# Key factors taken before the seventh combination, the first key transposes one group later, and one weight tile held for six low parts

## What is computed

```python
# layer 0
z = rms_norm(x) @ w_in                       # combined projection
a = pool_mixer(z[..., :512])                 # trailing means, 4 groups
for each of 4 heads:                         # differential attention
    q, k = rope(rms_norm(q)), rope(rms_norm(k))      # two maps of 64 channels each
    p1, p2 = softmax(mask(q1 @ k1.T)), softmax(mask(q2 @ k2.T))
    o = rms_norm((p1 - lam * p2) @ v) * (1 - lam_init)
x = x + concat(a, o) @ w_out
x = x + conv_ffn(x)                          # 1024 -> 2*2816 -> conv, gate -> 1024
# layer 1
q, k = silu(causal_conv(rms_norm(x) @ w_qk))
for each of 4 heads, 8 chunks of 128 tokens:         # mLSTM, matrix memory
    num  = (q @ k.T * decay_matrix) @ [v, 1] + (q * scale) @ state
    state = decay * state + k_weighted.T @ [v, 1]
h = rms_norm(num / max(|den|, exp(-m))) * sigmoid(o)
x = x + h @ w_out
x = x + conv_ffn(x)
```

## Time and profile before

| | |
|---|---|
| median of three runs | 2274.3 us (2273.61 to 2274.34) |
| the profiled execution's own time | 2274.28 us |
| its span, first to last instruction | 2272.5 us |
| TensorE busy | 2261.0 us, 99% |
| its weight loads | 1870.7 us, 82% |
| VectorE busy | 1190.7 us, 52% |
| ScalarE busy | 572.2 us, 25% |
| GpSimd busy | 882.0 us, 39% |

### The profile page before, as it was taken

One profiled execution on the slowest core, in us unless ns is written; L12 is line 12 of the kernel. 1 busy time (PEld: TensorE's weight loads), 2 busy tenths in 40 slices (PEclk: granted clock), 3 DMA queues, 4 the chain that ended last, 5 costly groups with the idle time before them and its releaser, 6 DMA issues.

```text
span 2272.5 us, 27216 instructions
## 1 busy us (share of the span) xinstructions
PE 2261.0 (99%) x10747; PEld 1870.7 (82%) x10747; DVE 1190.7 (52%) x1176; ACT 572.2 (25%) x888; POOL 882.0 (39%) x395
## 2 busy tenths in 40 slices
PE   9999999999999999999999999999999999999999
PEld 7777778888888888888888898788888888888887
DVE  7776763464554555545644144444545555554554
ACT  5555441221111111111344333422111111111110
POOL 1212226444334433344643333275344433443342
PEclk9999999999999999999999999999999999999999
DMA  5111121111111111111321111031111111111111
GB/s 195 56 47 47 33 92 57 47 47 49 54 46 46 46 54 47 46 47 53 115 79 56 35 59 65 21 135 45 51 47 46 46 55 46 46 46 52 50 47 74
DMA packets 38721, 132.29 MB, mean 58 GB/s; under 512 B 4912, under 2 KB 6768, under 8 KB 38640
## 3 DMA queue, kind: packets, MB, share of 16 engines
q1 hardware_dynamic: 35760, 122.24, 16.7%
q10 hardware_dynamic: 2880, 8.91, 1.0%
HBM read 118.26 MB, written 8.68 MB: 56 GB/s over the span
## 4 chain that ended last, share of the span: by engine, by line
PE 95%; DVE 3%; issue 1%; ACT 0%; DMA 0%; SPq 0%; ACTq 0%; DVEq 0%
PE pj L1367 42%; PE dn L1387 17%; PE pj L347 15%; PE pj L325 6%; PE pj L1860 3%; PE dn L1438 3%; PE dn L686 1%; PE pj L712 1%; PE pj L1438 1%; PE pj L506 1%; PE pj L696 1%; PE dn L1998 1%; PE dn L2007 1%; PE dn L1886 1%; PE pj L1886 1%
## 5 line engine op out<-in xcount | busy, mean ns | idle before, releaser
L1661 POOL TENSOR_TENSOR w_hi<-w_raw,ones 128x1024 fp32r<-128x1024 f32 x186 | 356.0, 1914 | 1329.9 <-PE pj L1367 564.0
L1663 POOL TENSOR_TENSOR w_lo<-w_raw,w_hi 128x1024 fp32r<-128x1024 f32 x186 | 468.3, 2518 | 14.6
L1491 DVE SCALAR_TENSOR_TENSOR ffn_y<-ffn_h,params,ffn_y 128x1024 f32<-128x1024 f32 x176 | 323.6, 1838 | 117.6 <-ACT ffn_y L1499 109.0
L1499 ACT ACTIVATE ffn_y<-ffn_h,params 128x1024 f32<-128x1024 f32 x88 | 109.6, 1245 | 886.6 <-DVE ffn_h L1480 886.6
L1480 DVE TENSOR_TENSOR ffn_h<-pj,rms_bc 128x1024 f32<-128x1024 f32 x88 | 107.8, 1225 | 365.5 <-PE pj L1367 351.9
L1540 DVE TENSOR_TENSOR res<-dn,res 128x1024 f32<-128x1024 f32 x144 | 176.1, 1223 | 115.4 <-PE dn L1387 115.4
L1367 PE MATMUL pj<-xb_hi,w_hi 128*128 128x512 f32 x704 | 216.9, 389 | 0.0
L1367 PE MATMUL pj<-xa_hi,w_hi 128*128 128x512 f32 x704 | 216.9, 389 | 0.0
L1367 PE MATMUL pj<-xb_hi,w_lo 128*128 128x512 f32 x704 | 216.7, 389 | 0.0
L1367 PE MATMUL pj<-xa_hi,w_lo 128*128 128x512 f32 x704 | 216.7, 389 | 0.0
L1367 PE MATMUL pj<-xa_lo,w_hi 128*128 128x512 f32 x704 | 216.7, 389 | 0.0
(11 more groups left out here) (321 smaller groups left out, 3550.4 us busy)
## 6 DMA issues: line engine op xcount, KB each, us to landing
w_raw<-weights SPq DMA_DIRECT2D x189, 512.0 KB, 3.5
x_first<-x_t SPq DMA_DIRECT2D x8, 512.0 KB, 9.8
res<-x_t SPq DMA_DIRECT2D x8, 512.0 KB, 6.8
scratch<-res ACTq DMA_DIRECT2D x8, 512.0 KB, 2.6
res<-scratch SPq DMA_DIRECT2D x8, 512.0 KB, 8.4
y_t<-res ACTq DMA_DIRECT2D x7, 512.0 KB, 2.6
q_turned<-q_raw SPq DMA_DIRECT2D x16, 128.0 KB, 2.3
k_turned<-k_raw SPq DMA_DIRECT2D x16, 128.0 KB, 2.3
```

The lines of the kernel that those rows point to most:

```text
L1491: dve.scalar_tensor_tensor(y[:, :], h[:, SH - lag:SH - lag + S], f.tap(j, m, q), y[:, :], ALU.mult, ALU.add).then_inc(taps[f.l], 1)
L1499: act.activation(f.y[m][:, :], f.h[m][:, SH:SH + S], ACT.Identity, bias=f.tap(j, m, 3), scale=f.tap(j, m, 2)).then_inc(center[f.l], 1)
L1661: pool.tensor_tensor(whi[:, w, :], raw[:, r, :], ones[:, 0:1].to_broadcast([P, D]), ALU.mult).then_inc(w_high, 1)
L1663: pool.tensor_tensor(wlo[:, w, :], raw[:, r, :], whi[:, w, :].bitcast(F32), ALU.subtract).then_inc(w_ready, 1)
```

## The change

Three edits, each independent of the others.

1. In `dve_mixer0`, for heads 0 to 2, `dve_KB` of half 0 of the next head moves from the head of block 7 (before its mask) to block 6, just before `dve_combine`.
2. In `pe_layer1`, `pe_KT` of head 0 is issued behind the seventh of the eight leading groups and no longer behind the sixth.
3. In `pool_layer1`, POOL waits, before it cuts tile T_OUT1 + 2, until `cat_lo[1]` has counted six low parts.

```diff
@@ dve_mixer0
                 for i in range(TB):
                     between, middle, after = block_groups(h, i)
-                    if i == TB - 1 and not last:
-                        dve_KB(dve, h + 1, 0)
                     dve_mask(dve, h, i)
@@
                     for G in between + middle + early:
                         extras(G)
+                    if i == TB - 2 and not last:
+                        dve_KB(dve, h + 1, 0)
                     dve_combine(dve, h, i)
@@ pe_layer1
                 for G in range(LEAD[h]):
                     pe_mix1_group(pe, *side1(h, G))
-                    if h == 0 and G == 5:
+                    if h == 0 and G == 6:
                         pe_KT(pe, 0)
@@ pool_layer1
+                if n == T_OUT1 + 2:
+                    pool.wait_ge(cat_lo[1], EARLY_CAT)
                 pool_cut(pool, n, n, 16 * (n // RAW_RING + 1))
```

## The result

The changed kernel takes 2278.24 us (median of 17 runs, 2277.81 to 2279.55) against 2273.89 us (17 runs, 2273.60 to 2274.34): 4.35 us more, a ratio of 1.002 with a 95% interval of 1.0014 to 1.0027. The forecast was 2276.6 us and "no change". The time lies inside the stated range, but the kernel did become slower, and the likeliest case missed 1.6 us of it. The profiled execution took 2279.19 us with a span of 2277.4 us, 4.9 us more than the 2272.5 of before; it is one of the slower of the 17.

A forecast was written before the change was run, and what follows sets the result against it. TensorE matmul work was taken to bound the kernel (95% of the chain that ended last). Terms 0 + 0.7 + 1.6 = +2.3 us on the profiled execution's 2274.28 gave 2276.6 us, range 2274.0 to 2278.4.

The forecast's parts named there:

- the likeliest case: Whole kernel: the terms for the three edits sum to +2.3 us, giving 2276.6 us; chance 60%.
- Part 1: Attention, heads 0 to 2: the 0.48 us wait for key factors goes, but the wait for `w_T` grows; sum 0.
- the term: Block 7 in attention: load about 0.35 us earlier, the 0.48 less about 0.1 of ordinary gap behind turns.
- Part 2: Start of the mLSTM, head 0: later key turns delay the chain to chunk 0's numerator, without slack; +0.7 us.
- Part 3: End of mLSTM head 3: low parts gain 1.3 us, POOL's cut in its new place costs 2.84; net +1.6 us.
- the 4.58 us of the earlier trace: Start of the program: time of the first 20 matmuls, 0.23 us each; about half taken as a clock fall's cost, +2.3.
- the hold pays: End of head 3: small DVE operations pass between POOL's two instructions, or POOL starts later; 2273.7 us, chance 10%.
- the factors or the late turns pay: Heads 0 to 2: 0.35 us three times, 2275.6 us; mLSTM start: chain has slack, 2275.5 to 2275.9; 10% each.
- the clock rival: Turns at head 3's end: after 4.4 us idle, first matmuls run at 1.2 GHz; +2.3 us, 2278.9; chance 10%.
- The bound of 4.5 us: Whole kernel: 0.2%, what a measurement can tell from no change; slower meant above 2278.8 us.
- The 5% for slower: Whole kernel above 2278.8 us: half of the clock rival's 10%, as its time lies just on that edge.

The follow-up runs named there:

- the fill: 18 extra matmuls, result not used, on TensorE's queue ahead of head 3's numerator's turns: changed kernel 2276.48 us, kernel before with three extra DVE operations 2277.04 us.
- the two filled kernels: Changed kernel, and kernel before with three extra DVE operations, each with 18 unused matmuls ahead of head 3's numerator's turns: 2276.48 and 2277.04 us.
- part 3 alone: Kernel before with only the weight tile held until six low parts are counted: 2277.94 us, ratio 1.0019.
- the longer wait: Kernel before with three extra DVE operations (about 3.1 us) ahead of the last operation on head 3's numerator, POOL unchanged: 2279.01 us, ratio 1.0024.
- the full change filled: Changed kernel with 18 extra matmuls, result not used, ahead of head 3's numerator's turns: 2276.48 us, ratio 1.0012.
- parts 1 and 2 alone: Kernel before with only the earlier key factors: 2273.89 us; kernel before with only the first key turns one group later: 2274.49 us.
- the second group: Unchanged kernel before, 33 runs timed beside the second group of experiment kernels: median 2273.96 us.
- both gains together: Kernel before with the tile held for all eight low parts and head 3's numerator's turns one group later: 2271.69 us, ratio 0.999.

## Why the prediction was wrong, step by step

- **Part 1, 0 us: right.** The gain was lost at the next wait, as said; that wait grew by 0.5 us, not 0.35, because no gap at all is left behind the turns of the key factors (the term had allowed 0.1). The time at which the wait ends did not move.
- **Part 2, +0.7 us: right.** 0.64 in the profiled execution, 0.68 by itself. The chain behind the turns had no slack.
- **Part 3, +1.6 us by the cut's new place: right in kind, 0.3 short.** The price of the cut was 6.02 - 3.14 = 2.88 us (2.84 forecast, from the end of head 1). The gain was 1.0 us and not 1.3. The mis-sized term is how much of chunk 7's earlier end reaches ACT's last high parts: 0.4 us by my estimate, 0.26 measured (they ended at 1462.97, which is 1462.3 without the shift of 0.67, against 1462.56 before). DVE stood 0.61 and 0.55 us for high parts and `m_out_gate` followed the last one by 1.56 us, not 1.5. With the clock held, the tile cost 2.0 us.
- **The clock: the step that failed.** I had worked out that TensorE would stand about 4.4 us, and it stood 4.41. That close a match was luck: without the shift the turns came 1.86 us late and not 1.5, and TensorE arrived 1.16 us early and not 1.5. I had a price as well: 2.3 us, half of the 4.58 us of the earlier trace rows. It was 2.35 in the profiled execution, 1.6 and 1.7 in two other traces, and 1.8 and 2.0 by the medians of two kernels with and without the fill. What the traces show in place of the earlier trace rows is half of the time that TensorE works at the low clock, 4.9 us in one and 3.4 in two. But I gave the fall 10% as a rival and left it out of the sum, because the granted clock was 1.00 with waits of up to 1.4 us and, as I read it, the trace held none above 1.48. It held one of 1.89 us on the weight loads, at 9.37 us, also at 1.00, but none near 4.4. That the rows did not show a fall was no evidence against it: they did not reach there. With the term in, the sum is 2274.28 + 0.7 + 1.6 + 2.3 = 2278.9 us, which is 0.7 us above the median of 2278.24, and the forecast would have been "slower". The rule of the Trainium skill ("TensorE: Matmul & The Clock Gate", Part 1: the idle engine's clock falls to the lower level) stood in the prediction and was the better guide. The traces agree in all three cases with an idle time above 4 us: 4.41, 4.41 and 4.67. All 38 runs of these three kernels have a mean granted clock of 0.998 or 0.999, and all 22 of the two filled kernels 1.000; and none of the 38 runs of the full change, of part 3 alone and of the longer wait was as fast as the median of its filled counterpart (part 3 alone is compared with the full change filled, which carries part 2's 0.68 us as well, so the comparison is generous to it).
- **The other rivals.** That the hold pays did not come about, because the small operations were held up just as at the end of head 1; with the tile held to the eighth low part it did pay, 1.0 us. That the factors or the late turns pay was refuted by parts 1 and 2 alone.
- **The range** of 2274.0 to 2278.4 held the median by 0.2 us at its upper end, by luck: it was drawn to leave out most of the clock rival, 2278.9, and that rival is what came, 0.7 us cheaper. The bound of 4.5 us, under which a change could not be told from none, was wrong too: 4.35 us is told apart, with an interval of 1.0014 to 1.0027. The 5% for slower rested on both.

Why POOL's cut stops DVE: the Trainium skill, "SBUF — State Buffer", section "SBUF: two separate sides", says that VectorE and GpSimd share one pair of ports, that an instruction holds it to its end, and that the other engine is fully blocked, where the VectorE operation reads two inputs from SBUF or uses both ports. The trace agrees: an operation on 8 columns took 2.25 us and ended with POOL's, while `m_out_gate`, one of whose inputs is in PSUM, took 1.22 us beside the cut and 1.21 without it.

## What to carry to other kernels

A transfer of work away from a critical stretch must name where it lands: a wait that is released by the last step of one critical stretch starts its work on the first step of the next. Of a wait on the bounding engine that grows, ask at once whether it is longer than any in the trace, and put the fall of its clock into the sum, not beside it; if the wait can't be shortened, real work moved into it is best, and even useless work gave back 1.8 and 2.0 us here. And when an order changes by one group, check each later point at which another engine's work is released by that engine's progress, not only the waits nearby.

## What the runs showed that I had not expected

That 18 matmuls whose result is thrown away made the changed kernel 1.8 us faster (2278.24 to 2276.48) and the kernel with the longer wait 2.0 us faster (2279.01 to 2277.04). That the clock can fall after the work has come back: in part 3 alone the turns began at 1471.06 at full clock, and the stretch from 1472 to 1474 had 0.58. That the same program takes 1.7 to 2.2 us more or less with this idle time, where 17 runs of the kernel before lie within 0.7: its executions fall into two groups, by a mean granted clock of 0.999 or 0.998, that do not overlap in time. What decides between the groups no run here shows. The mean was also 0.999 in one of the 33 runs of the kernel before in the second group (2275.16 us) and in one of both gains together (2272.95 us), each the slowest of its kernel: a fall can come, rarely, without the long idle time at the turns. And that the idle time of 1.39 us ahead of the turns, and that for the early low parts, could be had for 2.3 us in all by two edits of one line each.
